# Moving the turn-back of an attention unit's outputs behind the next unit's gate tile in a two-block fp32 kernel

## The reference, cut to what matters

```python
def nsa_mixer(h, w_in, w_out, k_pos, k_w1, k_w2, v_pos, v_w1, v_w2, table):
    q, kv, g, z = split_cols(h @ w_in, [NSA_WIDTH, 6 * NSA_KV_WIDTH, 3 * H, 3 * NSA_WIDTH])
    ...
    gates = jax.nn.sigmoid(g).reshape(B, S, 3, H, 1)
    zs = jax.nn.silu(z).reshape(B, S, 3, H, dh)
    o_cmp, p_cmp = nsa_compressed(q, kc, vc, table)
    sel = select_blocks(p_cmp, S)
    o_slc = nsa_selected(q, k_s, v_s, sel, table)
    o_win = nsa_window(q, k_w, v_w, table)
    o = jnp.stack([o_cmp, o_slc, o_win], axis=2)
    y = jnp.sum(gates * o * zs, axis=2).reshape(B, S, NSA_WIDTH)
    return y @ w_out
```

## Time and profile before

| what | us |
|---|---|
| median of 3 runs (lowest, highest) | 1374.87 (1374.79, 1375.23) |
| the profiled execution | 1374.61 |
| its span, first to last instruction | 1372.9 |
| TensorE matmul busy | 1333.3 (97%) |
| VectorE busy | 669.1 (49%) |
| ScalarE busy | 618.9 (45%) |
| GpSimd busy | 201.9 (15%) |
| mean granted TensorE clock, share of full | 0.995 |

### The profile page before, as it was taken

How to read it: one execution, slowest core, us unless ns; L and a number is a source line. 1 busy time by engine, 2 the same in 40 slices (tenths; PEclk the granted TensorE clock), 3 DMA queues, 4 the chain that set the end, 5 groups by cost and what they waited for, 6 DMA issues and landing times.

```text
span 1372.9 us, 18095 instructions
## 1 busy us (share of the span) xinstructions
PE 1333.3 (97%) x7245; PEld 1115.1 (81%) x7245; DVE 669.1 (49%) x1093; ACT 618.9 (45%) x961; POOL 201.9 (15%) x265
## 2 busy tenths in 40 slices
PE   5999999999999999999999999999999999999998
PEld 4887777777778887888888888788899998989876
DVE  4753444344444545434434344431256767776563
ACT  5254554446766424323323223244334666666232
POOL 1101333261000000000000000002712333332000
PEclk9999999999999999999999999999999999999999
DMA  8747534494424322322232322272512222222321
GB/s 170 111 111 115 77 78 81 105 196 99 61 54 59 93 96 71 110 92 92 95 105 89 109 92 92 92 218 77 131 39 67 81 70 70 63 85 78 99 71 62
DMA packets 94807, 128.81 MB, mean 94 GB/s; under 512 B 5840, under 2 KB 70464, under 8 KB 94737
## 3 DMA queue, kind: packets, MB, share of 16 engines
q1 hardware_dynamic: 88528, 108.70, 32.1%
q0 software_dynamic: 6064, 18.83, 5.2%
q10 hardware_dynamic: 144, 0.31, 0.1%
HBM read 124.94 MB, written 2.88 MB: 93 GB/s over the span
## 4 chain that ended last, share of the span: by engine, by line
PE 86%; DVE 5%; DMA 4%; POOL 2%; ACT 2%; issue 1%; SPq 0%; DVEq 0%
PE ps_g L581 44%; PE ps_g L604 13%; PE ps_z L604 12%; PE ps_z L1236 3%; PE ps_z L1273 2%; PE ps_t L1308 2%; DMA w_raw<-in_w_in 2%; DMA bc<-stat_rows_dram 2%; PE ps_t L1045 1%; PE ps_t L1083 1%; DVE w_lo L558 1%; PE ps_z L1097 1%; POOL y_f L1907 1%; PE ps_t L1158 1%; PE ps_z L1121 1%
## 5 line engine op out<-in xcount | busy, mean ns | idle before, releaser
L558 DVE TENSOR_TENSOR w_lo<-w_raw,w_hi 128x2048 fp32r<-128x2048 f32 (+1 forms) x96 | 220.9, 2302 | 302.0 <-ACT w_hi L550 302.0
L581 PE MATMUL ps_g<-act_hi,w_hi 128*128 128x512 f32 x784 | 309.4, 395 | 7.8 <-DVE act_lo L697 5.3
L581 PE MATMUL ps_g<-act_hi,w_lo 128*128 128x512 f32 x784 | 306.3, 391 | 0.0
L581 PE MATMUL ps_g<-act_lo,w_hi 128*128 128x512 f32 x784 | 305.9, 390 | 0.0
L550 ACT ACTIVATE w_hi<-w_raw 128x2048 fp32r<-128x2048 f32 (+1 forms) x96 | 182.2, 1898 | 210.1 <-PE ps_g L604 189.0
L581 PEld LDWEIGHTS ps_g<-act_hi,w_hi 128*128 128x128 f32 x784 | 147.7, 188 | 41.0 <-DVE w_lo L558 5.8
L581 PEld LDWEIGHTS ps_g<-act_hi,w_lo 128*128 128x128 f32 x784 | 147.5, 188 | 31.3
L581 PEld LDWEIGHTS ps_g<-act_lo,w_hi 128*128 128x128 f32 x784 | 147.6, 188 | 29.5
L581 PE MATMUL ps_g<-w_hi,act_hi 128*128 128x256 f32 x320 | 93.4, 292 | 0.0
L581 PE MATMUL ps_g<-w_lo,act_hi 128*128 128x256 f32 x320 | 90.3, 282 | 0.0
L581 PE MATMUL ps_g<-w_hi,act_lo 128*128 128x256 f32 x320 | 90.2, 282 | 0.0
(11 more groups left out here) (317 smaller groups left out, 2464.0 us busy)
## 6 DMA issues: line engine op xcount, KB each, us to landing
w_raw<-in_w_in SPq DMA_DIRECT2D x32, 1024.0 KB, 9.6
w_raw<-in_nsa_w_in SPq DMA_DIRECT2D x22, 1024.0 KB, 5.2
w_raw<-in_w_up SPq DMA_DIRECT2D x16, 1024.0 KB, 5.4
w_raw<-in_w_down SPq DMA_DIRECT2D x16, 1024.0 KB, 5.1
tile_t<-bias_rev_dram POOLq DMA_DIRECT2D x32, 256.0 KB, 3.0
bc<-stat_rows_dram POOLq DMA_DIRECT2D x24, 256.0 KB, 10.7
w_raw<-in_w_out SPq DMA_DIRECT2D x4, 1024.0 KB, 5.1
w_raw<-in_nsa_w_out SPq DMA_DIRECT2D x4, 1024.0 KB, 5.0
```

Of the source, the lines that this page charges most:

```text
L558: nc.vector.tensor_tensor(slab_view(w_lo[b], n), slab_view(w_raw[b], n), slab_view(w_hi[b], n).bitcast(F32), ALU.subtract).then_inc(lo_don ...
L581: mm = nc.tensor.matmul(o, stationary, moving, start=(k == 0 and j == 0), stop=(k == KT - 1 and j == 2))
```

## The change

`turn_back(u - 1)` leaves its place ahead of the transposes of unit u and goes behind the gate tile of unit u, behind the two waits for `probs_t` (`s_ta`, `s_td`) and right ahead of `values_of(u)`. With it the VectorE outputs of unit u - 1 go from the end of turn u - 1 to turn u, right behind the copy of `probs_t` and ahead of `split_lo` and of the evacuation. The ninth transpose waits for the outputs of unit u - 2 in place of those of u - 1. `rgate` gets two buffers, since the factor of u - 1 is now read a turn later. The number of instructions that compute stays the same on every engine.

```diff
-        rgate = sb("rgate", [P, TB])
+        rgate = sb("rgate", [P, 2, TB])
@@ TensorE
                     mm_tile(pe, N_NZ + 7, 3)
-                if u:
-                    turn_back(u - 1)
                 pe.wait_ge(s_probs, u + 1)
...
-                        if u and at == 1024:
-                            pe.wait_ge(s_out, u)
+                        if u >= 2 and at == 1024:
+                            pe.wait_ge(s_out, u - 1)
...
                 pe.wait_ge(s_ta, u + 1)
                 pe.wait_ge(s_td, u + 1)
+                if u:
+                    turn_back(u - 1)
                 values_of(u)
             turn_back(31)
@@ VectorE
+            def outputs(u):
+                h = u % HN
                 dve.wait_ge(s_back, u + 1)
                 for c, back in ((0, 1), (1, -1)):
...
-                        rgate[:, 2 * c:2 * c + 2].unsqueeze(2).broadcast_to([P, 2, DH]), ALU.mult)
+                        rgate[:, u % 2, 2 * c:2 * c + 2].unsqueeze(2).broadcast_to([P, 2, DH]), ALU.mult)
                 ins.then_inc(s_out, 1)
+
+            for u in range(32):
...
+                nc.vector.tensor_copy(probs_t[:, 512:CAUSAL], ps_t[:, 512:CAUSAL]).then_inc(s_td, 1)
+                if u:
+                    outputs(u - 1)
+                if u % 4 == 1:
+                    split_lo(dve, N_NZ + u // 4 + 1)
+                dve_evacuate(dve, order, N_NZ + u // 4, u % 4)
+                dve.wait_ge(s_probs, u + 1)
+                r = rgate[:, u % 2, :]
+                order.link(nc.vector.reciprocal(r, rsum[:, u % 2, :]))
+                order.link(nc.vector.tensor_tensor(r, r, gates_n[:, :, branch * HN + h], ALU.mult))
+            outputs(31)
```

More of the change, by code:

```diff
@@ L1813, in _ @@
                         o, src[:, ::back, :],
-                        rgate[:, 2 * c:2 * c + 2].unsqueeze(2).broadcast_to([P, 2, DH]), ALU.mult)
+                        rgate[:, u % 2, 2 * c:2 * c + 2].unsqueeze(2).broadcast_to([P, 2, DH]), ALU.mult)
                 ins.then_inc(s_out, 1)
+            for u in range(32):
+                h, branch = u % HN, 1 + u // HN
+                if u < 31:
+                    row_max(u + 1)
+                dve.wait_ge(s_t, u + 1)
+                if u:
+                    dve.wait_ge(s_pv, u)
+                nc.vector.tensor_copy(probs_t[:, 512:CAUSAL], ps_t[:, 512:CAUSAL]).then_inc(s_td, 1)
+                if u:
+                    outputs(u - 1)
[7 more added lines that the diff above has]
+            outputs(31)
             dve.wait_ge(s_out, 32)
```

## The result

The changed kernel takes **1398.14 us** (median of 4 runs, 1396.57 to 1400.22) against 1375.05 of the kernel before (4 runs, 1374.79 to 1376.14): ratio **1.0167**, 95% interval 1.015 to 1.0185. It is slower by 23.1 us; 25.3 had been forecast. A second session gave 1397.76 us and a ratio of 1.0151 (1.0134 to 1.0168).

A forecast was written before the change was run, and what follows sets the result against it. TensorE, 86% of the chain, was taken to bound the kernel. New waits of 22.0 us less 5.2 (+16.8) plus clock loss (+8.5) gave +25.3 us, about 1400 us; range 1380 to 1405.

The forecast's parts named there:

- The direction and the cause: Loop, turns with split_lo: later VectorE evacuation runs into GpSimd's L1969 and is blocked; slower by over 0.2%, chance 0.82.
- the one product in the earlier trace: VectorE's L1803 before the unit 14 wait: 1.02 us instead of 0.17, read as waiting for GpSimd's running instruction.
- no block counts: Rival, loop: only split_lo's 1.56 us lateness against the slack costs; -1.0 us, 1374, no change; chance 0.11.
- one block only: Rival, evacuation behind split_lo: held up by one GpSimd instruction only, gaps too short for the clock; +5.5 us, 1380; chance 0.16.
- The faster rival: Rival, split_lo turns: lateness fits under the gate tile, row maxima by T + 1.17; 5.2 us back, 1369.7; chance 0.07.
- The change did what it says: Opposite of a rival: other waits behind the ninth transpose keep the 5.2 us, result +30; chance called small.
- The sum of the waits: Loop, turn_back waiting for the copy of probs_t: 4 x 2.29 + 3 x 4.04 + 0.76 = 22.0 us, less 5.2 = +16.8.
- three blocks in a row of branch 1: Units 13, 17, 21: L837, L838 and the factor each wait for a GpSimd instruction; turn_back 4.04 us late each.
- The clock: TensorE's granted clock halves behind new gaps of 2.1 to 4.0 us: 5 x 1.70 = +8.5 us, bounds 0 and 11.9.
- Half of the four: Clock term: of the four gaps near 2.09 us, half counted as losing clock, besides the three long ones.
- Quiet turns: Loop turns without a wait: cost 0, gain 0, period stays 6.89 us; longer ones would show the prediction wrong.
- the outputs' waits: Loop, ninth transpose waiting for the outputs: 5.2 us in six waits, all expected to go.

The follow-up runs named there:

- the two orders: Changed kernel, in split_lo turns: rgate first, outputs last, evacuation before the key split; in others: outputs, rgate, evacuation. 1370.05 us, 0.9958 of the kernel before.

## Why the prediction was right, point by point

**The direction and the cause: right.** The page of the Trainium skill that the prediction weighed (SBUF — State Buffer, "Who interferes with whom") and the one product in the earlier trace rows decided it, and taking GpSimd out of the way takes the loss out. The rival *no block counts* falls with the 1.35 and 1.40 us of L837 and L838, the rival *one block only* with the second and third. The faster rival falls with the row maxima of unit 14 at T + 4.51, far behind its limit of T + 1.17. The change did what it says: no transpose waits for an output any more.

**The sum of the waits: 22.0 expected, 19.7 measured** (16.8 was that less 5.2).

| wait of `turn_back` in | expected | measured |
|---|---|---|
| units 2, 6, 10, 26 | 2.29 each | 2.16, 2.03, 2.16, 2.16 |
| units 14, 18, 22 | 4.04 each | 3.44, 3.58, 3.44 |
| unit 30 | 0.76 | 0.68 |

The places are the eight that were named. The term that was sized wrong is the three blocks in a row of branch 1. I let each blocked operation run its full 0.42 or 0.17 us behind the GpSimd instruction. In the profile L838 ends 0.28 us (as do all 35 evacuation operations held up in the ten profiles) and L1821 0.02 us behind what held them, and the next GpSimd instruction starts before they have ended, so three blocks cost 0.6 us less. Smaller: `split_lo` starts at T + 4.79, not 4.95, since the two transposes follow the gate tile at T + 3.97 and the outputs come 0.42 behind them.

**The clock: right in number, near in size, and the number with luck.** Five stretches were forecast and five came. They cost 7.7 us together, not 8.5: the loop is 27.3 us over its periods without a wait, and 19.7 of these are the waits above. Part of a stretch can lie in a gap or in slack. In the loops, of the 13 gaps of 2.0 to 2.35 us (idle time of the weight loads) in four profiles 6 were followed by a stretch (2 and 3 of 4 in the two of the changed kernel, 1 of 3 and 0 of 2 in two others), of the 6 gaps of 3.4 to 3.6 us all were, of the gaps up to 1.6 us none. "Half of the four" fits that, but it was a guess from one gap. The kernel before has a second gap of the same length, at a later norm, and the prediction did not read it:

```profile
889.30 0.55 PE L632 MATMUL ps_z<-cst,xn 128*128 128x128 f32 x3 [2.09 <-DVE xn L908]
```
```profile
889.00:894.00 5.00, 3.94 (x32) 3.44 (x32) 3.30 (x8) 1.96 (x6) 0.00 (x0) 1.00 0.00 0
```

The clock stays at 1.00 there. In all ten profiles the gap of the earlier trace rows (2.09 or 2.10 us) is followed by a stretch and this one (2.09 or 2.10 us) is not. So for gaps of about 2 us the length alone does not decide; what else does was not tried and stays open. The Trainium skill (TensorE: Matmul & The Clock Gate, "What's actually happening") has the clock fall after idleness. The trace agrees in so far as every stretch in the loop stands behind a gap.

**Quiet turns: a small miss.** I put them at cost 0 and named turns longer than 6.89 us as a sign of being wrong; a period is 6.91 us, which makes 0.6 us over the loop. The larger terms do not hang on it.

**Not expected: 2.2 us came back.** In the kernel before, the values waited for a late bias tile in three units (the copy in the earlier trace rows is one). I left that in the sum unchanged. In the kernel after, the bias tile takes at most 3.5 us to land, not 4.8 as before, and no unit pays for it.

So in the loop: + 19.7 + 7.7 + 0.6 - 4.8 (the outputs' waits, by the periods; 0.4 of the 5.2 lies behind the last first transpose) - 2.2 = + 21.0, against 20.8 measured. The 0.2 left is the first period, which has no `turn_back` in it any more (6.71 us instead of 6.93). All of these are read from the two profiles; why the bias tiles land earlier is unexplained.

## What to carry to other kernels

Before moving work on VectorE, draw GpSimd's instructions beside it and mark the VectorE operations with two SBUF operands, and here the negation of the maxima too: each that starts while GpSimd's subtractions run waits for the rest of that instruction, whatever its own size, and several in a row wait for several. Put the operations that read PSUM there and the others where GpSimd is idle. That order, not the place of the removed wait, was worth 28 us between the slowest and the fastest of these kernels. A block taken from one operation tends to reappear at the next one, so look for it in the whole turn before calling it gone.

## What the runs showed of the hardware that was not expected

- The two engines take turns. A VectorE operation that waits is served before GpSimd's next instruction, even if that one stands right behind: in all seven turns of the kernel after, L835 or L837 ran between GpSimd's two L1976. An operation of [128 x 4] then costs 1.04 to 1.06 us.
- The negation of [128 x 4] maxima, with one SBUF operand, is held up like those with two (0.85 us behind `q_lo`, and up to 1.15 us behind the key split in the two orders). The reciprocal of the same size (0.17 us beside L1976), the custom row maxima, the outputs and the copy of `probs_t` never are: in the loops of the ten profiles 49 reciprocals and 49 outputs start while a GpSimd subtraction runs, and take 0.16 to 0.17 and 0.27 to 0.29 us like the others.
- The late landings of the bias tile come mostly some 43 us apart in the kernels that keep the order of before: the late copies are in units 9, 15 and 21 of the kernel before, and in 5, 11, 17, 23 and 27 of the one with the rgate product early. The longest landing in the loop is 4.8 us in the three profiles with the order of before and 3.2 to 4.3 in the seven profiles with the changed order. What delays them was not tried and stays open.
